# A two-layer streaming encoder on one core: the layer norm of its convolution branch from one summed tile, forget gates in one pass of 16 columns, and a reordered start

## The reference

```
for i in range(2):
    x = LN(a*x + 0.5*swiglu(x, ffn_w_in[i,0], ffn_w_out[i,0]))     # 2816 hidden columns
    proj = x @ w_in[i] + b_in[i]                                   # 1024 -> 8968 columns
    h_c = mlstm(c_q, c_k, c_v, c_i, c_f) * sigmoid(c_o)            # c_i, c_f: 4 + 4 gate columns
    h_d = silu(layernorm(causal_dwconv31(d_a*sigmoid(d_g))))       # mean and variance over 512 channels
    merged = sum_n sigmoid(gates_n) * (h_n @ w_br[n])              # four branches
    x = LN(a*x + merged @ w_out[i])
    x = LN(a*x + 0.5*swiglu(x, ffn_w_in[i,1], ffn_w_out[i,1]))
    x = LN(a*x + sigmoid(x @ ple_gate_w[i] + b) * (p[i] @ ple_w[i]))
```

## Time and profile before

| what | value |
|---|---|
| median of 3 runs | 1436.04 us (1435.56 to 1437.43) |
| the profiled execution, its own time | 1432.55 us |
| its span in the profile | 1430.7 us |
| granted TensorE clock, mean over the span | 0.998 |
| PE, matmuls | busy 1409.7 us, 99% |
| DVE | busy 1067.0 us, 75% |
| ACT | busy 667.5 us, 47% |

### The profile page before, as it was taken

The page is one execution under the profiler, slowest core; times in us unless marked ns, Lnnn a source line. Parts: engine busy times, 40 slices in busy tenths (PEclk is TensorE's granted clock), DMA queues, the critical chain, the costliest instruction groups (busy, mean ns, idle before and its releaser), DMA issues.

```text
span 1430.7 us, 20859 instructions
## 1 busy us (share of the span) xinstructions
PE 1409.7 (99%) x8906; PEld 1260.8 (88%) x8906; DVE 1067.0 (75%) x1165; ACT 667.5 (47%) x653; POOL 53.7 (4%) x100
## 2 busy tenths in 40 slices
PE   8999999999999999999999999999999999999997
PEld 7888879999999888888878888899999998888885
DVE  4766686889887876666977666868997868666687
ACT  5444435663545444344444444447545464443441
POOL 0400000000000020000100000000000001000001
PEclk9999999999999999999999999999999999999999
DMA  7685545546554576564565555554456365655541
GB/s 266 222 256 187 177 149 176 177 132 218 161 169 148 192 230 224 186 202 156 173 234 179 200 195 193 177 174 151 155 199 175 97 228 181 225 176 199 203 158 59
DMA packets 168044, 263.18 MB, mean 184 GB/s; under 512 B 8958, under 2 KB 101456, under 8 KB 167952
## 3 DMA queue, kind: packets, MB, share of 16 engines
q1 hardware_dynamic: 163616, 249.66, 52.4%
q0 software_dynamic: 4336, 12.20, 2.8%
HBM read 260.77 MB, written 1.05 MB: 183 GB/s over the span
## 4 chain that ended last, share of the span: by engine, by line
PE 92%; DVE 5%; ACT 1%; DMA 0%; SPq 0%; issue 0%; DVEq 0%; ACTq 0%
PE ps L1373 20%; PE ps L1277 18%; PE ps L1279 18%; PE ps L1278 18%; PE ps L1375 10%; PE ps L1485 3%; DVE big L929 2%; PE ps L1303 1%; PE ps L1308 1%; PE ps L1305 1%; DVE wlo L782 1%; PE ps L1344 1%; ACT whi L549 1%; DMA raw<-in_ffn_w_in 0%; DVE big L865 0%
## 5 line engine op out<-in xcount | busy, mean ns | idle before, releaser
L782 DVE TENSOR_TENSOR wlo<-raw,whi 128x2048 fp32r<-128x2048 f32 x230 | 521.9, 2289 | 219.0 <-ACT whi L549 218.8
L549 ACT CAST whi<-raw 128x2048 fp32r<-128x2048 f32 x230 | 438.0, 1911 | 373.7 <-PE ps L1279 242.6
L1373 PE MATMUL ps<-xhl,whi 128*128 128x512 f32 x1280 | 446.9, 392 | 2.6 <-DVE S L797 2.4
L1375 PE MATMUL ps<-xhl,wlo 128*128 128x256 f32 x1280 | 357.9, 280 | 0.0
L1277 PE MATMUL ps<-xhl,whi 128*128 128x256 f32 x1056 | 298.2, 282 | 0.0
L1278 PE MATMUL ps<-xhl,whi 128*128 128x256 f32 x1056 | 296.1, 280 | 0.0
L1279 PE MATMUL ps<-xhl,wlo 128*128 128x256 f32 x1056 | 296.1, 280 | 0.0
L1373 PEld LDWEIGHTS ps<-xhl,whi 128*128 128x128 f32 x1280 | 240.3, 188 | 56.8 <-DVE S L797 2.7
L1375 PEld LDWEIGHTS ps<-xhl,wlo 128*128 128x128 f32 x1280 | 240.5, 188 | 1.4
L1277 PEld LDWEIGHTS ps<-xhl,whi 128*128 128x128 f32 x1056 | 199.0, 188 | 1.3 <-issue 1.0
L1278 PEld LDWEIGHTS ps<-xhl,whi 128*128 128x128 f32 x1056 | 199.0, 188 | 0.1
(11 more groups left out here) (249 smaller groups left out, 1493.8 us busy)
## 6 DMA issues: line engine op xcount, KB each, us to landing
raw<-in_ffn_w_in SPq DMA_DIRECT2D x172, 512.0 KB, 5.0
raw<-in_w_in SPq DMA_DIRECT2D x140, 512.0 KB, 4.5
raw<-in_ffn_w_out SPq DMA_DIRECT2D x88, 512.0 KB, 4.2
raw<-in_w_br SPq DMA_DIRECT2D x32, 512.0 KB, 5.0
raw<-in_w_out SPq DMA_DIRECT2D x16, 512.0 KB, 4.4
raw<-in_ple_gate_w SPq DMA_DIRECT2D x16, 512.0 KB, 4.7
gv<-in_ln_g POOLq DMA_DIRECT2D x8, 512.0 KB, 4.4
b_bc<-in_ln_b POOLq DMA_DIRECT2D x8, 512.0 KB, 6.1
```

What stands on the lines that cost most here:

```text
L549: nc.scalar.copy(whi[:, slot, :], raw[:, source, :]).then_inc(whi_made, 1)
L782: nc.vector.tensor_tensor(wlo[:, slot, :], raw[:, source, :], whi[:, slot, :].bitcast(F32), ALU.subtract).then_inc(wlo_made, 1)
L1373: nc.tensor.matmul(ps[:, 2 * q + u, :], w[:, k, u, P * q:P * q + P], xhl[:, :, 4 * kk + k, :], start=kk == 0 and k == 0, stop=False, skip_ ...
L1375: ins = nc.tensor.matmul(ps[:, 2 * q + u, 256:512], v[:, k, u, P * q:P * q + P], xh[:, 4 * kk + k, :], start=False, stop=kk == 1 and k == ...
```

## The change

- The mean and the variance of branch D each come from one `ones_d` matmul on `csum`, a 128 x 256 tile that DVE sums from the four channel tiles in two additions (`channel_sum`). The mean moves from the end of the gate of step 5 to the middle of the gate of step 6, the variance to its end. On DVE the last 32 taps move from one block in step 4 to 8 behind step 4's product and 24 in step 5; the sum stands ahead of the split of chunk 20; in step 6 the subtraction, the second sum and the rest of the norm stand around the splits of chunks 21 and 22. ACT's square moves from the end of step 5 to step 6.
- The forget gates use one 16-column tile `wifs` (high 8, low 8) against the high and the low part of x: 8 x 2 matmuls a layer; DVE adds the two halves afterwards, in one more small instruction.
- The first half of chunk 0 is cast and split ahead of x tile 0; SP issues x tile 1 behind chunk 1.
- In step 0 of every FFN one split moves from ahead of product 1 to behind it, on ACT and on DVE.
- `turn_x` becomes two `turn_half`s of 4 transposes; where a fresh x tile 1 is turned, the first stands ahead of the last four matmuls of tile 0. In the first FFN of layer 1 the order stays as it was.

```diff
+            def channel_sum(a, signal):
+                pairs = big[:, 0:512].rearrange("p (m t) -> p m t", m=2)
+                link(nc.vector.tensor_tensor(pairs, a[:, 0:2, :], a[:, 2:4, :], ALU.add))
+                nc.vector.tensor_tensor(csum, pairs[:, 0, :], pairs[:, 1, :], ALU.add).then_inc(signal, 1)
...
@@ DVE, branch steps @@
-                    if s == 5:
+                    if s == 6:
                         dve.wait_ge(mean_done, l + 1)
                         nc.vector.tensor_tensor(yc, yc, ps[:, 6, 0:256].unsqueeze(1).to_broadcast([P, KW, T]),
                                                 ALU.subtract).then_inc(d_made, 1)
+                        dve.wait_ge(dsq_made, l + 1)
+                        channel_sum(s4(1), vsum_made)
+                        los(base + gate_chunk(s, 1) + RING - 1)
+                        dve.wait_ge(dvar_done, l + 1)
...
+                        branch_low(1, s4(1), NB * l + 4)
+                        los(base + gate_chunk(s, 1) + RING + 1)
+                        continue
                     los(base + gate_chunk(s, 1) + RING)
+                    if s == 5:
+                        conv_taps(l, CONV_OPS)
+                        dve.wait_ge(conv_step, CONV_OPS * (l + 1))
+                        channel_sum(yc, ysum_made)
...
-                    if s == 4:
-                        conv_taps(l, CONV_OPS)
...
+                        if e == 4:
+                            conv_taps(l, 8)
@@ PE, branch steps @@
+                        if s == 6 and kk == 1:
+                            pe.wait_ge(ysum_made, l + 1)
+                            mm(ps[:, 6, 0:256], ones_d[:, :], csum).then_inc(mean_done, 1)
...
-                    if s == 5:
-                        pe.wait_ge(conv_step, CONV_OPS * (l + 1))
-                        for m in range(KW):
-                            ins = mm(ps[:, 6, 0:256], ones_d[:, :], yc[:, m, :], start=m == 0, stop=m == KW - 1)
-                        ins.then_inc(mean_done, 1)
+                    if s == 6:
+                        pe.wait_ge(vsum_made, l + 1)
+                        mm(ps[:, 7, 0:256], ones_d[:, :], csum).then_inc(dvar_done, 1)
...
-                    if s == 5:
-                        pe.wait_ge(dsq_made, l + 1)
-                        for m in range(KW):
-                            ins = mm(ps[:, 7, 0:256], ones_d[:, :], s4(1)[:, m, :], start=m == 0, stop=m == KW - 1)
-                        ins.then_inc(dvar_done, 1)
@@ PE, forget gates @@
-                    ins = mm3(ps[0:8, 6, 0:256], wif_hi[:, k, :], wif_lo[:, k, :], xh[:, k, :], xl[:, k, :],
-                              start=k == 0, stop=k == KD - 1)
+                    mm(ps[0:16, 6, 0:256], wifs[:, k, :], xh[:, k, :], start=k == 0, stop=False)
+                    ins = mm(ps[0:16, 6, 0:256], wifs[:, k, :], xl[:, k, :], start=False, stop=k == KD - 1)
@@ DVE, step 0 of an FFN @@
-                    los(g + RING + (j > 0))
+                    los(g + RING + (1 if j > 0 else -1))
                     if j == 0:
                         product(n, 0)
+                        los(g + RING)
+                        product(n, 1)
                         los(g + RING + 1)
-                        product(n, 1)
@@ PE, fresh x tile @@
+                    if kk == 1 and between is not None:
+                        between()
                     pe.wait_ge(xlo_made, 4 * n + 2 * t + kk + 1)
```

More of the change, by code:

```diff
@@ L609, in head @@
                                raw[:, i // 2, 1024 * (i % 2):1024 * (i % 2) + 1024]).then_inc(whi_made if i % 2 else head_hi, 1)
+            head(0)
             split_x(0, 0)
-            for i in range(4):
+            for i in range(1, 4):
                 head(i)
@@ L696, in _ @@
                     if s == 6:
+                        act.wait_ge(d_made, l + 1)
+                        nc.scalar.activation(s4(1), yc, ACT.Square).then_inc(dsq_made, 1)
                         act.wait_ge(dvar_made, l + 1)
@@ L983, in head_low @@
                                         ALU.subtract).then_inc(wlo_made if i % 2 else head_lo, 1)
+            head_low(0)
             low_x(0, 0)
-            for i in range(4):
+            for i in range(1, 4):
                 head_low(i)
@@ L1402, in ffn, with first_half @@
                     pe.wait_ge(h_made, 2 * n0)
-                fresh_tokens(c0, 0, 0, version, n0 == 0, signal=gate0_done)
-                if n0 == 0:
-                    pe.wait_ge(x_in[1], 16)
-                turn_x(version, 1, xtok)
+                def first_half():
+                    if n0 == 0:
+                        pe.wait_ge(x_in[1], 16)
+                    turn_half(version, 1, 0)
+                early = n0 == 0 or version % 4 != 0
+                fresh_tokens(c0, 0, 0, version, n0 == 0, signal=gate0_done, between=first_half if early else None)
+                if not early:
+                    first_half()
+                turn_half(version, 1, 1)
                 fresh_tokens(c0, 1, 1, version, n0 == 0)
```

82 lines of the change are left out of this document (40 added, 42 removed).

## The result

The changed kernel takes 1426.43 us (median of 6 runs, 1423.77 to 1428.84) against 1435.93 us for the kernel before (6 runs, 1435.56 to 1437.43). The ratio is 0.9934 with a 95% interval of 0.9922 to 0.9946, so 9.5 us less, between 7.8 and 11.2. Timed again later (experiment 3), it is 8.6 us less, between 6.7 and 10.3. The profiled execution took 1424.88 us for a span of 1422.7; beside the profiled 1432.55 and 1430.7 of before that is 8.0 us less in the span.

What follows compares the result with a forecast made beforehand. PE, busy in 99% of the span, was taken as the bound. Forget gates 1.9, halves of x 1.9, start 3.5, mean and variance 3.5 sum to 10.8 us off the median 1436.04: 1425.2 us, range 1421.5 to 1429.5.

Steps and rivals of the forecast that it cites:

- likeliest case: All four parts act, with a wait of 0.3 to 2 us a layer before output projection; 1423.5 to 1427, chance 0.53.
- Forget gates: 8 fewer matmuls of 0.12 us in each of two layers; 1.9 us saved, the extra DVE instruction costed at nothing.
- Halves of x: Input projection and second FFN of both layers: first half's cast runs under four matmuls, saving 4 x 0.49 = 1.9 us.
- the first half comes late: Lower bound for turning x in halves: if its first half is late each time, nothing is saved.
- The start: Three edits in a row at the program's start, up to step 0; 3.5 us saved, bounds 1.5 and 4.5.
- (a): At the start, x tile 1's 512 KB leave the way of chunk 1; 1.0 to 1.66, say 1.3 us saved.
- (b): At the start, x is turned in halves; 0.49 us saved.
- (c): Step 0 of the first FFN: second product ahead of chunk 4's split; 1.7 of PE's 2.35 us wait saved.
- Mean and variance: PE's work falls 2.9 us a layer; a 1.2 us wait before the output projection leaves 1.75, 3.5 in two.
- The walk along DVE and ACT: Layer 0, step 4's product to merged's low part: that ends at 474.8, PE is done at 473.6, waits 1.2 us.
- Rival 2: No new wait before the output projection, as DVE has unseen slack; 1422.8 us, chance 0.17.
- Rival 3: ACT's table loads behind the branch hold it twice their 1.28 us; 1427.8, with other delays 1427 to 1430; chance 0.21.

Runs made afterwards that it cites:

- experiment 3: The changed kernel timed and profiled once more with no edit; 1425.42 us, ratio 0.9940 to the kernel before.
- experiment 8: The changed kernel with the first half of chunk 0 cast and its low part taken behind x again; 1426.20 us, ratio 0.9936.
- experiment 6: The kernel before with only the turning of x in halves added; 1434.41 us, ratio 0.9994.
- Experiment 9: The changed kernel with the transfer of x tile 1 issued ahead of chunk 1 again; 1428.78 us, ratio 0.9949.
- Experiment 1: The changed kernel with DVE's products of steps 6 and 7 and their low parts of merged moved ahead of splits; 1422.79 us, ratio 0.9914.

## Why the prediction was right, and where it was not

The forecast was 1425.2 us in a range of 1421.5 to 1429.5, the result 1426.43. Its likeliest case is the one that came: all four parts act and a new wait stands in front of the output projection. By its own steps, in the profiled spans:

- **Forget gates**, 1.9 us: 0.9 in each layer, as forecast. The slower pace of the matmuls behind it, 0.9 us in two layers in the first profile, was in no term.
- **Halves of x**, 4 x 0.49: measured 0.55 three times, and -0.11 in layer 1, where the bound "the first half comes late" was met. 1.5 us in place of 1.9.
- **The start**, 3.5 us: 3.65. The terms: (a) and (b) together, read at the start of tile 1, 1.57 for 1.79; (c) 2.08 for 1.7, since the wait that I thought might stay in part went down to 0.25. The possible hold-up of 0.6 us by the new order of the first half did not show (experiment 8). (b) was taken as its own gain; experiment 6 shows that without (c) the wait behind it swallows it. The Trainium skill, DMA: Bandwidth & Descriptors, section Queues, rings and completion order, says that completion is not first-in-first-out per issuing engine, and I took that as a reason against (a). The same section says that each DMA engine consumes its descriptors in ring order, so it does not say that the order of issue is worth nothing. Experiment 9 shows that here it mattered, by 1.15 us of 1.3 forecast.
- **Mean and variance**, 3.5 us: the gains at the output projections are 6.57 - 4.67 = 1.90 and 7.42 - 5.89 = 1.53, together 3.4. But two sizes inside were off, in opposite directions, and that the sum held is luck. PE's own work fell by about 3.2 us a layer, not 2.9: what the two single matmuls replace was 4.4 us for 4.12, and they cost 0.43 and 0.70, together 1.13 for 1.24. And the wait was 470.00 - 467.91 - 0.12 = 1.97 us in layer 0 and 1.70 in layer 1, not 1.2. The walk along DVE and ACT held almost exactly: shifted by the 4.94 us by which the variance's matmul came earlier, it has the product of step 6 at 465.06, and the row says 465.08; from there to the end of the low part it has 4.83, and it was 4.82. What failed is PE's pace beside it: I let a chunk take 5.76 us, which is 48 matmuls at 120.0 ns, the pace at this place in the one profile of before. In the changed kernel's profile it was 117.3 in layer 0 (5.63 a chunk) and 118.7 in layer 1. At 117.3, PE arrived 0.5 us earlier in four chunks, and so waited that much longer; where a profile has 120.0 there (experiment 3, layer 0) the wait by the same count is 469.45 - 467.88 - 0.12 = 1.45 us, near the 1.2. That the gain in layer 0 is 1.90 and not 1.53 as in layer 1 comes from the pace too: before ran at 120.0 there and at 118.7 in layer 1, and it had no wait at this place to hide that.
- **What was missing**: the clock. No term and no rival had it. It took 1.53 us in the profiled execution, behind the very wait that I had forecast. With it the sum is 3.7 + 1.5 + 1.8 - 0.9 + 3.4 - 1.5 = 8.0 us, which is the measured difference of the spans, where I had 10.8.
- **From the profile to the median.** I set the 10.8 us against the median and not against the profiled execution. The medians differ by 9.5 us, the profiled spans by 8.0. The profiled execution of before had no stretch at low clock, and its time is 3.4 us below the median beside it; the one of after had one. The timed runs have no traces, but each has its mean granted clock, and the time goes with it: of the 57 times of before beside the experiments, the four with 0.998, as in the profile, average 1432.8 us, and the seventeen with 0.995 average 1436.3. The mean clock over all 57 is 0.996, as it is over the eleven times of the changed kernel and in its profile. So before's profile was an execution with less low clock than usual, and with the 1.5 us of that one stretch the 8.0 become 9.5. That I put 10.8 on the median and came within 1.2 us of it has this accident on its side.

Rival 2 (no new wait) is not what happened. Experiment 1 makes it happen, but that its 1422.79 us equals the 1422.8 of the rival is chance: the kernel before took 1434.43 beside it and not 1436.04. Rival 3 asked for a later chain by a longer hold of the table loads. The walk cannot test that, since it took the stretch with the last load from the profile of before as a whole, whatever is in it. The rows can: that load starts at 461.18, 0.02 us behind the cast ahead of it (459.26 + 1.90), and ACT's next instruction 0.01 behind its end. No drain of about 1380 ns, as the Trainium skill, ScalarE: Activation LUTs, section What ACT_TABLE_LOAD costs, has it, shows on either side.

Open: what sets the pace of the 256-column matmuls (117.3, 118.7 or 120.0 ns) for tens of microseconds at a time; and whether the length of the wait by itself makes the clock fall, or the pace ahead of it has a part in that.

## What to carry to other kernels

When work moves from the bounding engine to another one, walk that other engine's chain to the next place where the bounding engine needs it, with the bounding engine's own pace measured to a per cent and in more than one execution, since the wait is a small difference of large numbers. Then put what the bounding engine waits for ahead of work that has cover: that order on DVE was worth 4.3 us here by the ratios, 2.9 to 3.5 by the profiled spans, between a third and a half of the whole change. And price a wait of TensorE of 1.8 us or more, as they stood here, not at its length but at that and up to 1.5 us behind it.

## What the runs showed of the hardware

- Behind waits of 1.80 us in front of the output projection (5 of 5), and of 2.78 and 2.80 us in step 0 (2 of 2), TensorE ran at a granted clock of 0.50 to 0.54 for about 3 us, losing 1.5 us; behind waits of 1.28 to 1.55 us (7 of 7) it kept its clock. Behind 2.33 to 2.35 us in step 0 it kept it twice, and once lost it, 1.2 us after it had resumed. (The waits of 1.80 all stand behind the fast pace of the next point.) Such stretches also stand at places with several short gaps (about 290, 720, 990 us) in some executions and not in others: 0 to 3 in each of the profiles here.
- At a granted clock of 1.00, the 256-column fp32r matmuls of the same program start 117.3, 118.7 or 120.0 ns apart on average, for tens of microseconds at a time, and which it is at a given place differs between executions and between the layers of one (the table of experiment 3). On 190 matmuls that is up to 0.51 us.
- A table load of ACT takes 1.28 us. Where nothing is waited for, as at 461.18 in the profile of before, it starts 0.02 us behind the end of the instruction ahead of it, and the next starts 0.01 us behind its end.
- The same transfer at the start of the program is ready for its cast at 6.25 us in one execution and at 8.06 in another.
